# Layer norms A and B: squares about the first tile's mean gathered during the output projection, token sums by TensorE, stores issued by SyncE

## The reference

```python
h, hc = x, ctx                      # 1024 tokens and 256 context tokens, width 1024
for i in range(2):
    shift, scale, gate = split(silu(c) @ w_ada[i] + b_ada[i])
    u = h * (1 + scale) + shift
    y, yc = mixer_a(u, uc, ...) if i == 0 else mixer_b(u, uc, ...)
    h = layer_norm(ALPHA * h + gate * y, ln_g[i], ln_b[i])
    if i == 0:
        hc = layer_norm(ALPHA * hc + gate_c * yc, ln_g[i], ln_b[i])

def layer_norm(x, g, b):
    mu = mean(x, axis=-1)
    var = mean(square(x - mu), axis=-1)
    return (x - mu) * rsqrt(var + LN_EPS) * g + b
```

## Time and profile before

| | before |
|---|---|
| median of 3 runs | 3244.74 us (3243.88 to 3247.97) |
| span of the profiled execution, first to last instruction | 3236.3 us |
| TensorE busy | 3109.7 us (96%) |
| VectorE busy | 1999.7 us (62%) |
| ScalarE busy | 1299.9 us (40%) |
| GpSimd busy | 759.8 us (23%) |
| mean granted clock of TensorE | 0.988 of full speed |

### The profile page before, as it was taken

One profiled execution on the slowest core, in us unless ns is written; L12 is line 12 of the kernel. 1 busy time (PEld: TensorE's weight loads), 2 busy tenths in 40 slices (PEclk: granted clock), 3 DMA queues, 4 the chain that ended last, 5 costly groups with the idle time before them and its releaser, 6 DMA issues.

```text
span 3236.3 us, 47842 instructions
## 1 busy us (share of the span) xinstructions
PE 3109.7 (96%) x18134; PEld 2578.9 (80%) x18134; DVE 1999.7 (62%) x3834; ACT 1299.9 (40%) x2340; POOL 759.8 (23%) x324
## 2 busy tenths in 40 slices
PE   9999999999999989999899999999899999999987
PEld 6888888777777767877799889888677778777765
DVE  5676677555565657975755555556755555655555
ACT  5534443444444440022444444440344444454412
POOL 3223332322222213543211121113112112111221
PEclk9999999999999999999999999999999999999999
DMA  3111111111111137521200010153201111100141
GB/s 118 46 40 46 46 59 46 60 59 53 53 53 53 64 146 298 220 79 52 91 30 30 31 43 30 46 203 130 78 21 51 45 51 45 51 32 33 67 161 76
DMA packets 64828, 237.79 MB, mean 73 GB/s; under 512 B 7008, under 2 KB 10080, under 8 KB 63600
## 3 DMA queue, kind: packets, MB, share of 16 engines
q1 hardware_dynamic: 31680, 115.91, 9.9%
q10 hardware_dynamic: 32944, 119.10, 9.7%
HBM read 185.11 MB, written 49.87 MB: 73 GB/s over the span
## 4 chain that ended last, share of the span: by engine, by line
PE 79%; DVE 9%; ACT 5%; issue 2%; DVEq 2%; DMA 1%; ACTq 1%; SPq 0%
PE ps L1304 21%; PE ps L189 13%; PE ps L360 9%; PE ps L2223 7%; PE ps L1368 5%; PE ps L1334 4%; PE ps L1350 4%; PE ps L891 3%; PE ps L482 3%; PE ps L868 2%; PE ps L133 2%; DVE fox_l L1455 1%; PE ps L852 1%; DVE wa_l L941 1%; PE ps L853 1%
## 5 line engine op out<-in xcount | busy, mean ns | idle before, releaser
L210 POOL TENSOR_TENSOR w_hi<-raw,small 128x1024 fp32r<-128x1024 f32 x160 | 334.9, 2093 | 2393.7 <-PE ps L1304 1099.3
L212 POOL TENSOR_TENSOR w_lo<-raw,w_hi 128x1024 fp32r<-128x1024 f32 x160 | 424.8, 2655 | 22.8
L1304 PE MATMUL ps<-nb_u_hi,w_hi 128*128 128x512 f32 (+1 forms) x640 | 249.2, 389 | 6.1 <-DVE nb_q_lo L2470 4.2
L1304 PE MATMUL ps<-nb_u_hi,w_lo 128*128 128x512 f32 (+1 forms) x640 | 246.6, 385 | 0.0
L1304 PE MATMUL ps<-nb_u_lo,w_hi 128*128 128x512 f32 (+1 forms) x640 | 245.7, 384 | 0.0
L1466 DVE TENSOR_TENSOR nb_pt_lo<-ps,nb_pt_hi 128x512 fp32r<-128x512 f32 x208 | 143.9, 692 | 144.2 <-ACT nb_pt_hi L1393 143.9
L360 PE MATMUL ps<-u_hi,w_hi 128*128 128x512 f32 x528 | 212.8, 403 | 5.9 <-ACT silu_h L539 2.6
L1304 PE MATMUL ps<-u_hi,w_lo 128*128 128x512 f32 x512 | 208.9, 408 | 0.0
L360 PE MATMUL ps<-u_hi,w_lo 128*128 128x512 f32 x528 | 208.6, 395 | 0.0
L360 PE MATMUL ps<-u_lo,w_hi 128*128 128x512 f32 x528 | 208.4, 395 | 0.0
L1304 PE MATMUL ps<-u_hi,w_hi 128*128 128x512 f32 x512 | 208.3, 407 | 0.0
(11 more groups left out here) (357 smaller groups left out, 8027.8 us busy)
## 6 DMA issues: line engine op xcount, KB each, us to landing
raw<-in_w_stream SPq DMA_DIRECT2D x160, 512.0 KB, 3.3
h_sb<-in_w_ada ACTq DMA_DIRECT2D x16, 1024.0 KB, 5.0
nf_b<-nf_rows ACTq DMA_DIRECT2D x16, 512.0 KB, 4.4
nb_bias<-in_rel_bias ACTq DMA_DIRECT2D x16, 448.0 KB, 3.8
y_parts<-wa_y_hi ACTq DMA_DIRECT2D x8, 640.0 KB, 3.0
y_parts<-wa_y_lo ACTq DMA_DIRECT2D x8, 640.0 KB, 4.2
la_out_yh<-y_parts SPq DMA_DIRECT2D x8, 640.0 KB, 10.0
la_out_yl<-y_parts SPq DMA_DIRECT2D x8, 640.0 KB, 11.1
```

The costliest lines, as they stand in the source:

```text
L210: pool.tensor_tensor(w_hi[:, s, :], raw[:, s, :], zero, ALU.add)
L212: pool.tensor_tensor(w_lo[:, s, :], raw[:, s, :], w_hi[:, s, :].bitcast(F32), ALU.subtract).then_inc(w_ready, 1)
L1304: mm = pe.matmul(ps[:, b:b + ch["n"]], w(slot, k), u[:, k, ch["c0"]:ch["c0"] + ch["n"]], start=k == 0 and p == 0, stop=k == KT - 1 and p == 2)
```

## The change

The variance is no longer made from x minus the mean. With c the mean of the token over the first 128 channels, the kernel gathers the squares of x - c, tile by tile, while the projection runs, and takes var = E[(x - c)^2] - (mean - c)^2. In detail:

- TensorE broadcasts the mean of tile 0 over its 128 channels into banks 6 and 7, after tile 2 of the projection for the context (A alone; ScalarE copies it to `c_ctx`) and after tile 3 for the latents. The loop over the tiles is written out.
- VectorE takes x - c of each tile (`from_centre`), ScalarE squares it in place, VectorE adds it to `acc2` (`add_square`). Tiles 0 and 1 are done behind tile 3, tiles 2 to 4 behind tile 4, then each behind its own tile, the last in parts. The last tile of h goes into `acc` too.
- TensorE makes sums per token (a token on each partition) of `acc` and `acc2`; the variance is then three instructions on 8 or 10 columns.
- Of the eight subtractions of the mean (`centre`) some are moved behind the variance: in A two before it, one before the diagonal, five after; in B two, one, two, and three inside `scale`.
- The stores of A's h to DRAM come after the root. The stores of the output are issued by SyncE (`send_b`), without a drain on ScalarE.
- The window mask of layer A leaves `consts` and is loaded by itself as `wa_win`.

```diff
 def pe(self, pe, mixer):
-    with pe.Fori(0, KT // 2) as i:
-        for m in range(2):
...
+    for k in range(KT):
+        m = k % 2
...
+        if k == 2:
+            pe.wait_ge(self.added, self.base + 1)
+            if self.cols == TC:
+                broadcast_means(pe, self.h[:, 0, T:TC], C, 6, True, True).then_inc(self.early_mean, 1)
+        if k == 3:
+            pe.wait_ge(self.early_copied, 1)
+            broadcast_means(pe, self.h[:, 0, 0:T], T, 6, True, True).then_inc(self.early_mean, 1)
-    pe.wait_ge(self.summed, (KT - 1) * (self.l + 1))
     pe.wait_ge(self.gated, 1 + self.base + KT - 1)
-    broadcast_means(pe, self.acc, self.cols, 0, True, False)
-    pe.wait_ge(self.added, self.base + KT)
-    broadcast_means(pe, self.h[:, KT - 1, :], self.cols, 0, False, True).then_inc(self.mean_sum, 1)
-    pe.wait_ge(self.gated, 1 + self.base + KT)
-    for k in range(KT):
-        pe.wait_ge(self.sq_set, self.base + k + 1)
-        broadcast_means(pe, self.sq[:, k % 2, :], self.cols, 3, k == 0, k == KT - 1
-                        ).then_inc(self.sq_sum, 1)
+    parts = self.chunks
+    for p, (t, n) in enumerate(parts):
+        pe.wait_ge(self.last_summed, self.parts0 + p + 1)
+        self.token_sums(pe, self.acc, t, n, 0)
+        if p == len(parts) - 1:
+            pe.wait_ge(self.gated, 1 + self.base + KT)
+            broadcast_means(pe, self.acc, self.cols, 3, True, True).then_inc(self.mean_sum, 1)
+        pe.wait_ge(self.squared, self.parts0 + p + 1)
+        mm = self.token_sums(pe, self.acc2, t, n, 1)
+    mm.then_inc(self.token_sum, 1)
     spread_rows(pe, self.cols, self.diag, 0, 3 + self.l, 18)
...
+def token_sums(self, pe, src, t, n, b):
+    for j in range(t // P, (t + n) // P):
+        mm = pe.matmul(ps[:, b * CH + j:b * CH + j + 1], src[:, j * P:(j + 1) * P], ones_mean[:, 0:1],
+                       start=True, stop=True)
+    return mm

 def act(self, act, mixer):
+    def squares(j, cols=slice(0, self.cols), n=0):
+        act.wait_ge(self.early_set, self.early0 + j + n + 1)
+        buf = self.t2[:, j % 2, cols]
+        nc.scalar.activation(buf, buf, ACT.Square).then_inc(self.early_sq, 1)
     residual(1)
     if self.l == 0:
+        act.wait_ge(self.early_mean, 1)
+        nc.scalar.copy(self.c_ctx[:], ps[:, 6 * CH:6 * CH + C]).then_inc(self.early_copied, 1)
         next_ada(1)
     residual(2)
+    for j in range(5):
+        squares(j)
     residual(3)
+    squares(5)
     if self.l == 0:
         act.wait_ge(ada_done, PAIRS_ADA + 4)
         load_bias(act, 0)
-    for k in range(KT):
-        act.wait_ge(self.centred, self.base + k + 1)
-        if k >= 2:
-            act.wait_ge(self.sq_sum, self.base + k - 1)
-        nc.scalar.activation(self.sq[:, k % 2, :], self.h[:, k, :], ACT.Square).then_inc(self.sq_set, 1)
-        if self.l == 0:
-            act.dma_start(h_dram[k, :, 0:T], self.h[:, k, 0:T]).then_inc(b_stored, 16)
+    squares(6)
+    for p, (t, n) in enumerate(self.chunks):
+        squares(KT - 1, slice(t, t + n), p)
     load_sqrt_table(act)
     act.wait_ge(stat_var, 2 + self.l)
     standard_deviations(act, self.cols, None, small[:, 2:3])
+    if self.l == 0:
+        for k in range(KT):
+            act.wait_ge(self.centred, self.base + k + 1)
+            act.dma_start(h_dram[k, :, 0:T], self.h[:, k, 0:T]).then_inc(b_stored, 16)

 def dve(self, dve, meanwhile=None):
     dve.memset(self.acc[:], 0.0)
+    dve.memset(self.acc2[:], 0.0)
...
+    def from_centre(j, cols=slice(0, self.cols)):
+        dve.drain()
+        buf = self.t2[:, j % 2, :]
+        lat = slice(cols.start, min(cols.stop, T))
+        if lat.stop > lat.start:
+            ins = dve.scalar_tensor_tensor(buf[:, lat], ps[:, 6 * CH + lat.start:6 * CH + lat.stop], -8.0,
+                                           self.h[:, j, lat], ALU.mult, ALU.add)
+        if cols.stop > T:
+            ins = dve.scalar_tensor_tensor(buf[:, T:TC], self.c_ctx[:], -8.0, self.h[:, j, T:TC],
+                                           ALU.mult, ALU.add)
+        ins.then_inc(self.early_set, 1)
+    def add_square(j, cols=slice(0, self.cols), n=0):
+        dve.wait_ge(self.early_sq, self.early0 + j + n + 1)
+        dve.drain()
+        return dve.tensor_tensor(self.acc2[:, cols], self.acc2[:, cols], self.t2[:, j % 2, cols], ALU.add)
+    def centre_tokens():
+        dve.wait_ge(self.early_mean, 2 + l)
+        for j in range(self.cols // P):
...
+            dve.tensor_tensor_reduce(self.t2[:, 1, j * P:(j + 1) * P], src, ident, 8.0, small[:, 0:1],
+                                     ALU.mult, ALU.add, self.c_tok[:, j:j + 1])
     for k in range(KT):
+        if k == KT - 1:
+            add_square(KT - 2)
...
+            if k == KT - 1:
+                dve.drain()
+                dve.tensor_tensor(self.acc[:, cols], self.acc[:, cols], self.h[:, k, cols], ALU.add
+                                  ).then_inc(self.last_summed, 1)
+                from_centre(k, cols)
+                if part == 0:
+                    add_square(k, cols).then_inc(self.squared, 1)
...
+        if k == 3:
+            centre_tokens()
+            from_centre(0)
+            from_centre(1)
+            add_square(0)
+            add_square(1)
+        elif k == 4:
+            from_centre(2)
+            from_centre(3)
+            add_square(2)
+            from_centre(4)
+            add_square(3)
+            add_square(4)
+        elif k == 5:
+            from_centre(5)
+            add_square(5)
+        elif k == 6:
+            from_centre(6)
+    for p, (t, n) in list(enumerate(self.chunks))[1:]:
+        add_square(KT - 1, slice(t, t + n), p).then_inc(self.squared, 1)
     dve.drain()
     dve.wait_ge(self.mean_sum, l + 1)
-    for k in range(KT):
-        dve.tensor_tensor(self.h[:, k, :], self.h[:, k, :], self.flat(0), ALU.subtract
-                          ).then_inc(self.centred, 1)
+    for k in range(2):
+        self.centre(dve, k)
+    n = self.cols // P
+    dve.wait_ge(self.token_sum, l + 1)
+    dve.tensor_tensor(self.d_tok[:], ps[:, 0:n], self.c_tok[:], ALU.subtract)
+    dve.drain()
+    dve.tensor_tensor(self.d_tok[:], self.d_tok[:], self.d_tok[:], ALU.mult)
+    dve.drain()
+    dve.tensor_tensor(std[:, 0:n], ps[:, CH:CH + n], self.d_tok[:], ALU.subtract).then_inc(stat_var, 1)
+    self.centre(dve, 2)
+    inverse_diagonals(dve, self.cols, self.diag, 3 + l)
+    for k in range(3, KT if l == 0 else 5):
+        self.centre(dve, k)
     if meanwhile:
         meanwhile(dve)
-    dve.wait_ge(self.sq_sum, self.base + KT)
-    token_variances(dve, self.cols, 3, self.diag)
-    inverse_diagonals(dve, self.cols, self.diag, 3 + l)
+    dve.drain()
     dve.wait_ge(stat_row, 3 + l)

 def scale(self, dve):
     for k in range(KT):
+        if k >= 5:
+            self.centre(dve, k)
+            dve.drain()
         dve.scalar_tensor_tensor(self.h[:, k, 0:T], self.h[:, k, 0:T],
...
 def store_b(act):
...
-                                     bias=vecs[:, V_LNB + KT + k:V_LNB + KT + k + 1])
-                act.drain()
-                act.dma_start(a["out"][k], layer_b.h[:, k, :]).then_inc(out_stored, 16)
-            act.wait_ge(out_stored, 16 * KT)
+                                     bias=vecs[:, V_LNB + KT + k:V_LNB + KT + k + 1]).then_inc(out_set, 1)
+        def send_b(sp):
+            for k in range(KT):
+                sp.wait_ge(out_set, k + 1)
+                sp.dma_start(a["out"][k], layer_b.h[:, k, :]).then_inc(out_stored, 16)
+            sp.wait_ge(out_stored, 16 * KT)
```

More of the change, by code:

```diff
@@ L1975, in ready @@
                         (self.y_early, 32 * len(mixer.early)) if self.by_parts else last)
-                with pe.Fori(0, KT // 2) as i:
-                    for m in range(2):
-                        free = [w for b in (range(3) if m == 0 else range(3, 8)) for w in mixer.free(b)]
-                        project(pe, i * 2 + (self.n_out + m), m, self.yh, self.yl,
-                                self.span(3 * m, free + [(self.gated, i * 2 + (self.base + m))]), self.chunk,
-                                ready=ready, tiles_outer=m == 0 and not self.by_parts,
-                                late=last if self.by_parts else None)
@@ L1986, in pe @@
-                pe.wait_ge(self.summed, (KT - 1) * (self.l + 1))
-                pe.wait_ge(self.gated, 1 + self.base + KT - 1)
-                broadcast_means(pe, self.acc, self.cols, 0, True, False)
-                pe.wait_ge(self.added, self.base + KT)
-                broadcast_means(pe, self.h[:, KT - 1, :], self.cols, 0, False, True).then_inc(self.mean_sum, 1)
-                pe.wait_ge(self.gated, 1 + self.base + KT)
-                for k in range(KT):
-                    pe.wait_ge(self.sq_set, self.base + k + 1)
-                    broadcast_means(pe, self.sq[:, k % 2, :], self.cols, 3, k == 0, k == KT - 1
-                                    ).then_inc(self.sq_sum, 1)
+                for k in range(KT):
+                    m = k % 2
```

(13 more changed lines are left out.)

34 lines of the change are left out of this document (26 added, 8 removed).

## The result

The changed kernel takes 3262.6 us (median of 4 runs, 3257.6 to 3263.4), the kernel before 3245.3 (3243.9 to 3248.0): ratio 1.0056, 95% interval 1.0044 to 1.0068, that is 17.3 us slower (14 to 22). The forecast was 3257, range 3244 to 3264. Its sign and its mechanism hold. Of its 12.7 us the parts are found again, some with errors that nearly cancel, and one part of 4.5 us was missing.

What follows compares the result with a forecast made beforehand. TensorE was busy 96% of the span, but VectorE's list, blocked by GpSimd, would bound both projection ends. 8.9 - 0.3 + 1.1 + 1.5 + 1.5 = 12.7 took the span 3236.3 to 3249.0; plus 8.4: 3257 us, range 3244 to 3264.

Steps and rivals of the forecast that it cites:

- What goes: Path behind each mean: A from 29.65 to 18.3 us, gain 11.35; B from 22.67 to 8.0, gain 14.7.
- What comes, A: Projection A: longer VectorE list plus blocking makes the mean 20.3 us later; net for A +8.9 us.
- The undisturbed list: VectorE's work in projection A from tile 3 on without blocking: 63.2 us, ending at 2284.0.
- the blocking: VectorE and GpSimd instructions with SBUF operands shut each other out during the projections: 12.6 us in A, 7.8 in B.
- What comes, B: Projection B: list 53.3 us plus blocking 7.8, mean 14.4 us later; net for B -0.3 us.
- Tail: From scale's first product to the end: three subtractions move in, stores go to SyncE; 17.7 us, +1.1 with start-up.
- Clock: TensorE waiting before the means: matmuls slowed by a partly fallen clock, +1.5 us in each layer.
- cold TensorE: Rival: matmuls before both means run at half clock, 3260.5 us; chance 0.16.
- My own sign of being wrong: TensorE's clock: the prediction would be wrong if it fell for much longer than one of the old falls.
- Start of layer B's products: Layer B's first matmuls may lose 1.7 us after rest; a later 4.2 us VectorE wait can absorb it: 0.
- Nothing: Smaller consts, wa_win load, later stores, unrolled loop, second memset: no cost; uncovered, each at most 0.3 to 1.3 us.
- Around the span: Outside the profiled span: the 8.4 us by which the median of the runs exceeds it stay unchanged.

Runs made afterwards that it cites:

- run 1: The kernel before, with SyncE issuing the eight stores of the output: ratio 0.9997.
- run 2: The kernel before, with the window table loaded by a transfer of its own into wa_win: ratio 1.0006.
- run 3: The changed kernel with layer B's norm, scale and order of subtractions as in the kernel before; layer A's change and SyncE's stores stay: ratio 1.0038.
- run 6: The kernel before, with GpSimd filling w_hi and w_lo of projections A and B with zeros instead of splitting weights: ratio 1.0001.
- run 5: The changed kernel, with GpSimd filling w_hi and w_lo of projections A and B with zeros instead of splitting weights: ratio 1.0009.
- run 4: The changed kernel with layer A's norm as in the kernel before; layer B's change, its late subtractions and SyncE's stores stay: ratio 1.0002.
- run 8: The changed kernel with filler matmuls keeping TensorE busy in every wait before the means of both layers: ratio 1.0049.
- run 7: The changed kernel with 28 added matmuls before the first token sum, 4 before the last in each layer, 34 behind A's spread: ratio 1.0052.
- run 11: The kernel before, with TensorE's loop over the eight tiles of projection A written out: ratio 1.0002.
- run 12: The changed kernel with squares of h itself, TensorE's loops as in the kernel before, B's subtractions all ahead of scale: 3231.8 us, ratio 0.9964.
- run 10: The changed kernel with squares of h itself, added behind each tile, without first-tile mean or differences from it: 3238.3 us, ratio 0.9981.
- run 9: The changed kernel with all eight subtractions of layer B's mean ahead of scale, as in the kernel before: ratio 1.0049.

## Why the prediction was right, point by point

- **What goes.** Behind A's mean 17.85 us (18.3 forecast), behind B's 8.8 (8.0; the spread is waited for 1.06 us). Right. In B the old path was not always the 22.67 of the forecast: it is 24.4 in runs 1, 2, 3 and 6.
- **What comes, A.** The undisturbed list ends 107.8 us behind the first tile (run 5; 104.8 forecast), the blocking adds 7.9 (12.6 forecast): 115.7 in sum, 117.4 forecast. Two errors that nearly cancel. The list was too short, 2 of the 3.0 us because eleven additions of 1280 columns take 1.49 and not about 1.3 each (the STT of 1280 columns in the earlier trace rows had 1.50 already). The blocking by its rows is 2.0 for each of the sums of tiles 3 and 4, 3.6 for squares in tile 4 (6.69 less two of 1.49 and a drain), 1.1 each in tiles 5 and 6, where I had 1.5 and 2.9: 9.8, of which 1.9 fell into waits that are there anyway. Mean +21.5 (20.3 forecast with 1.5 more for the clock): that it fits so well is in part luck.
- **What comes, B.** Blocking 7.9 in the list (7.8). B as a whole +0.1 (run 4) and +1.9 (changed kernel) against the mean of the old norm, forecast 1.2 with the clock.
- **Tail.** +1.0 (1.1); SyncE's stores give 2.1 (2.6), the moved subtractions take 3.1 (3.7 by my figures).
- **Clock.** At least 2.3 in A and 1.4 in B (run 8) instead of 1.5 each. The sum of 3.0 was near the 3.7, the picture behind it was not: I took the clock at half for about half the time, and it was at 0.50 from 2287.0 to 2307.5 without a break, as the rival "cold TensorE" had it. My own sign of being wrong, a clock that falls for much longer than before, came: 20.5 us in each layer instead of 3.4. The page that I named ("TensorE: Matmul & The Clock Gate" of the Trainium skill, Part 1) says that an idle TensorE falls to 1.2 GHz; the trace agrees (0.50 after the projection's end), and the bursts between did not bring the clock back.
- **Start of layer B's products: 0.** Right, and run 7 shows that the wait behind takes it up.
- **Nothing.** The step that failed: I put the unrolled loop, the second memset and the later stores at nothing, and at 1.3 us each at most. With layer A's change projection B starts 4.5 us later (run 3). The measured 17.3 us exceed the 12.7 of the sum by 4.6: this term is the size of the miss, and the other errors cancel.
- **Around the span.** "8.4 us by which the median exceeds the span, unchanged" was not a fixed cost: execution by execution the time is the span plus 1.9 (3263.35 and 3261.5). By that the profiled execution of the kernel before took 3238.2 us, 7.1 below the median of its runs. The forecast was not hurt, since both medians carry the same scatter.

By means over the profiles: A +9.6 (140.4 less 130.8), B's start +4.5, B +1.0, tail +1.0, together 16.1, beside 17.3 (14 to 22) by the medians.

**Open.** Whose code the q8 block is can be read from the traces: from 2190 to 2270, during projection A, q8 brings four blocks in each of the eight kernels that have TensorE's loop over A's tiles written out, and none in the six that have it as a loop. So q8 carries TensorE's code, and a longer or shorter list of TensorE's instructions shifts all later blocks. Where the block before or at the last stores of y falls changes with it: 9.8 us before the attention's last matmul in the kernel before, 5.9 before it in runs 11 and 12, 4.5 behind it in the changed kernel. Run 11 thus shows that writing out the loop alone shifts the block, but not far enough. Run 12 differs from run 10 in the loops and in B's subtractions, and I did not separate the two; run 9, with the subtractions back and the loops open, keeps the late start (25.2 us), which speaks for the loops. That the block causes the late start is not shown: it rests on their coming together, seen in 14 of 14 executions, and no run moved the block alone.

## What to carry to other kernels

Work put beside a running projection is free only while the engine's list, with all the time in which GpSimd's instructions block it, ends before the last tile; here a list shorter by a quarter (squares of h itself leave out the reductions and differences, 14.8 of the forecast's 63.2 us) and spread over all tiles turned +17 us into -4, and -11 with the loops kept. How much the shorter list gives and how much the spreading was not separated. What the end of the long stage sets off on another engine (here the next split of weights) meets just the instructions on the critical path (run 10). And a stretch is compared over several executions before it is explained: 6 us of difference ahead of the change were scatter.

## What the hardware showed

- Short bursts did not bring the clock back: with token sums of about 2 us every 0.3 to 1.6 us TensorE stayed at 0.50 until 2307.5. In run 8, where fillers left at most 0.7 us of rest at a time, the clock was 1.00 to 2291 and 0.80 to 0.85 in the next 10 us, and the broadcast took 2.40 us.
- Whether the clock falls differs between executions. The same 32 matmuls of B's squares took 13.97 us in the kernel before (granted clock 1.00 over them) and 15.67 in run 1 (0.89 from 3207 to 3223), behind the same wait of 2.49 us. Run 11 has 13.97 too, runs 2, 3 and 6 have 15.67.
```profile
3199.35 13.97 PE L133 MATMUL ps<-lb_sq,ones_mean 128*128 128x512 f32 x32 [2.49 <-ACT lb_sq L2033]
```
```profile
3207.08 15.67 PE L133 MATMUL ps<-lb_sq,ones_mean 128*128 128x512 f32 x32 [2.49 <-ACT lb_sq L2033]
```
- A load of instructions may not always be hidden. The Trainium skill ("Runtime: NRT & Kernel Launch", section "Instruction fetch mechanics") has each sequencer fetch blocks of 16 KiB on a DMA queue of its own and calls the cost mostly hidden. The packets of 0.02 MB on q8 agree with the first. Against the second stand store issues of 0.86 to 1.16 us instead of 0.33 beside the block in the changed kernel and runs 5, 9 and 10, and the late starts; that the block is their cause is not shown.
